# Two mixture-of-experts layers in fp32: expert weights multiplied unsplit, on column tiles of TensorE

## The reference

```
def expert_choice_ffn(h, w_router, w1, w3, w2):
    cap = max(1, EC_CAPACITY * T // N_EXPERTS)
    aff = jax.nn.softmax((h @ w_router).astype(jnp.float32), axis=-1)
    gate, idx = lax.top_k(jnp.swapaxes(aff, 1, 2), cap)
    xin = jax.vmap(lambda hb, ib: hb[ib])(h, idx)
    hid = jax.nn.silu(jnp.einsum('becd,edf->becf', xin, w1)) * jnp.einsum('becd,edf->becf', xin, w3)
    y = jnp.einsum('becf,efd->becd', hid, w2) * gate[..., None].astype(h.dtype)
    return jax.vmap(lambda yb, ib: jax.ops.segment_sum(
        yb.reshape(-1, D), ib.reshape(-1), num_segments=T))(y, idx)
```

## Time and profile before

| | us |
|---|---|
| median of 3 runs (4937.42 to 4945.94) | 4940.01 |
| the profiled execution | 4945.59 |
| its span, first to last instruction | 4943.9 |
| PE busy | 4181.3 |
| DVE busy | 2556.5 |
| ACT busy | 1902.5 |
| POOL busy | 1369.3 |
| granted TensorE clock, mean | 0.903 |
| raw loads, of 750.91 MB moved in all | 384 x 1 MB |

### The profile page before, as it was taken

How to read it: one execution, slowest core, us unless ns; L and a number is a source line. 1 busy time by engine, 2 the same in 40 slices (tenths; PEclk the granted TensorE clock), 3 DMA queues, 4 the chain that set the end, 5 groups by cost and what they waited for, 6 DMA issues and landing times. The chain is left out here.

```text
span 4943.9 us, 57028 instructions
## 1 busy us (share of the span) xinstructions
PE 4181.3 (85%) x23791; PEld 2752.6 (56%) x23791; DVE 2556.5 (52%) x3270; ACT 1902.5 (38%) x2614; POOL 1369.3 (28%) x814
## 2 busy tenths in 40 slices
PE   8988869999978956388996688887898998898998
PEld 4546546566644434277884556654445764455763
DVE  2215436777763037655534399898555331455321
ACT  2114216676643147333340276675114211123211
POOL 2200027686650012200002186676100210001210
PEclk9999979999999977657896799998999999999999
DMA  5330126888863138633322198897211221301321
GB/s 214 128 116 31 54 74 244 300 314 291 280 242 142 43 137 279 197 96 89 89 79 109 69 351 321 314 340 284 99 43 50 106 83 34 108 34 62 108 79 41
DMA packets 410482, 750.91 MB, mean 152 GB/s; under 512 B 67280, under 2 KB 143424, under 8 KB 410224
## 3 DMA queue, kind: packets, MB, share of 16 engines
q1 hardware_dynamic: 398816, 705.14, 40.8%
q0 software_dynamic: 11408, 42.13, 2.4%
HBM read 684.26 MB, written 62.94 MB: 151 GB/s over the span
## 5 line engine op out<-in xcount | busy, mean ns | idle before, releaser
L75 POOL TENSOR_TENSOR whl<-raw,whl 128x512 fp32r<-128x512 f32 x384 | 947.3, 2487 | 489.6 <-ACT whl L72 489.1
L75 DVE TENSOR_TENSOR whl<-raw,whl 128x1536 fp32r<-128x1536 f32 x384 | 871.2, 2292 | 135.7 <-ACT whl L72 132.5
L72 ACT ACTIVATE whl<-raw 128x2048 fp32r<-128x2048 f32 x384 | 730.4, 1915 | 288.7 <-PE ps L62 174.4
L62 PE MATMUL ps<-whl,xp 128*96 128x512 f32 (+2 forms) x2560 | 652.4, 406 | 77.9 <-DVE whl L75 41.5
L62 PEld LDWEIGHTS ps<-whl,xp 128*96 128x96 f32 (+2 forms) x2560 | 409.9, 165 | 301.1 <-DVE whl L75 73.1
L62 PE MATMUL ps<-c,hT 128*128 128x512 f32 (+2 forms) x1024 | 420.0, 565 | 5.1 <-ACT hT L72 2.8
L62 PE MATMUL ps<-whl,hidT 128*96 128x512 f32 (+2 forms) x1280 | 337.8, 415 | 60.9 <-DVE whl L75 45.1
L62 PE MATMUL ps<-wp,hp 128*128 128x512 f32 x1536 | 360.3, 396 | 20.2 <-DVE wp L75 20.2
L62 PE MATMUL ps<-a,nahT 128*128 128x512 f32 x768 | 338.5, 597 | 5.6 <-ACT nahT L72 5.2
L62 PEld LDWEIGHTS ps<-wp,hp 128*128 128x128 f32 x1536 | 290.8, 189 | 87.1 <-issue 27.3
L62 PEld LDWEIGHTS ps<-c,hT 128*128 128x128 f32 x1024 | 192.2, 192 | 200.0 <-issue 192.3
(11 more groups left out here) (468 smaller groups left out, 6251.9 us busy)
## 6 DMA issues: line engine op xcount, KB each, us to landing
raw<-in_moe_w_dram SPq DMA_DIRECT2D x384, 1024.0 KB, 5.2
c<-in_w_in_dram SPq DMA_DIRECT2D x28, 2048.0 KB, 9.2
a<-in_ada_w_dram SPq DMA_DIRECT2D x16, 2048.0 KB, 13.1
b<-in_ada_w_dram SPq DMA_DIRECT2D x8, 2048.0 KB, 9.9
a<-in_na_w_qkv_dram SPq DMA_DIRECT2D x6, 2048.0 KB, 19.1
c<-in_w_branch_dram SPq DMA_DIRECT2D x16, 512.0 KB, 4.2
c<-in_w_out_dram SPq DMA_DIRECT2D x4, 2048.0 KB, 9.0
c<-in_w_ple_gate_dram SPq DMA_DIRECT2D x4, 2048.0 KB, 8.0
```

The costliest lines, as they stand in the source:

```text
L62: return self.e.matmul(out, lhsT, rhs, start=start, stop=stop, skip_group_check=True) if self.e is not None else self
L72: return self.e.activation(*a, **k) if self.e is not None else self
L75: return self.e.tensor_tensor(*a, **k) if self.e is not None else self
```

## The change

Both layers now run one `moe_experts`, with the same quarters of 256 x 1024, and `pairs_experts` goes. The weights are not split: PE multiplies raw itself, in fp32, and the ring of raw (six tiles in layer 0, twelve in layer 1) is freed by PE's own count. The 64 latent tokens of an expert are multiplied by two column halves at once: columns 0 to 511 of the weight into partitions 0 to 63 and columns 512 to 1023 into partitions 64 to 127 of one bank. The 32 context tokens of layer 0 take four such tiles of 32 partitions and 256 columns each. With that, hid is 128 x 512 and no fold is needed, and POOL has nothing in the stage. Weighing by slot and by gate row comes into one operation on DVE (Yw, Ycw); Yw is split for an fp32r scatter, context results stay fp32 (Yc, Sc). The residual is loaded into acc ahead, so the scatter adds onto it. acc is the tile mx (layer 0) or hx (layer 1), into which the route loaded x before; the last groups are of two experts each. Layer 0's result stays in mx: `rw_norm` reads it there, rw_project's SP stores it to xl for the readout, and mx is then used again as kk and for scratch. The route of layer 0 now makes wslot too.

```diff
-class Halves:
+class Quarters:
...
-        self.src = [w[ex][h * 512:h * 512 + 512, n * 512:n * 512 + 512] for what, ex in self.order
-                    for n in range(2) for w in ws[what] for h in range(2)]
+        self.src = [w[ex][256 * q:256 * q + 256, :] for what, ex in self.order for w in ws[what] for q in range(4)]
...
-            e.wait_ge(*P.dve.at(self.name, 'low', u - self.nr))
-            e.wait_ge(*P.pool.at(self.name, 'low', u - self.nr))
-        n = self.src[u].shape[1]
-        to = self.raw[:, u % self.nr].rearrange("p a b -> p (a b)").rearrange("p (k n) -> p k n", n=n)
-        e.dma_start(to, self.src[u].rearrange("(k p) n -> p k n", p=128)).then_inc(*self.sig[u % self.nr].inc(self.name, u))
+            e.wait_ge(*self.P.pe.at(self.name, 'quarter', u - self.nr))
...
-                e.wait_ge(*P.dve.at(name, 'low', u))
-                out = P.psum[0:M, bank[p], :]
-                for k in range(4):
-                    kk = 4 * h + k
-                    if k == 3:
-                        e.wait_ge(*P.pool.at(name, 'low', u))
-                    e.matmul(out, x[:, kk, 0], hi(u)[:, k, :], (h, k) == (0, 0), False)
-                    e.matmul(out, x[:, kk, 0], lo(u)[:, k, :], False, False)
-                    ins = e.matmul(out, x[:, kk, 1], hi(u)[:, k, :], False, (h, k) == (1, 3))
...
+def moe_experts(P, I, l, mod, srcs, acc, name, chunks, nch, H, xinT, affT, posn, pix, bcc, posr, wslot, idr):
...
+                e.wait_ge(*H.loaded(u))
+                W = H.raw[:, u % H.nr]
                 for k in range(2):
+                    kk = 2 * q + k
+                    for t in range(2):
+                        X = xinT[:, kk, ex, 0:64] if kind == 'A' else hidT[:, ex % 2, kk]
+                        ins = e.matmul(P.psum[half(t), bank[0], :], X, W[:, k, cols(t if kind == 'A' else swap(t, ex))], kk == 0, kk == 7)
+                    for j in range(4 if two else 0):
+                        X = xinT[:, kk, ex, 64:96] if kind == 'A' else hicT[:, ex % 2, kk]
+                        ins = e.matmul(P.psum[part(j), bank[1], 0:256], X, W[:, k, blk(j)], kk == 0, kk == 7)
                 ins.then_inc(*P.pe.inc(name, 'quarter', u))
...
+                e.scalar_tensor_tensor(out=Yw[:], in0=P.bank(name, 'p', 'B', ex, 0), scalar=wslot[:, ex:ex + 1], in1=gl[:, ex % 2, :],
+                                       op0=MUL, op1=MUL).then_inc(*P.dve.inc())
...
-        e.wait_ge(*s_res.at(name, 'residual'))
-        for s, ch in enumerate(chunks):
-            for i in ch:
-                e.wait_ge(*P.dve.last())
-                e.tensor_tensor(acc[:, i, :], acc[:, i, :], xo[:, nch + s], MUL).then_inc(*P.dve.inc())
-                e.wait_ge(*P.dve.last())
-                e.tensor_tensor(acc[:, i, :], acc[:, i, :], xo[:, i], ADD).then_inc(*P.dve.inc(name, 'result', i))
...
+                if u == H.nr + 1:
+                    fence(P, e, k_('route'))
                     e.wait_ge(*gate_out(P, l, 1))
+                    for t in range(2):
+                        for ex in range(2):
+                            n = swap(t, ex)
+                            e.dma_start(gl[half(t), ex, :], bc(mod[l, 0, 5120 + n * 512:5632 + n * 512], 64)).then_inc(*s_gate.inc())
+                    for j in range(4 if two else 0):
+                        e.dma_start(gc[part(j), :], bc(mod[l, 1, 5120 + j * 256:5376 + j * 256], 32)).then_inc(*s_gate.inc())
+                    s_gate.name(name)
+                    for s, (src, ch) in enumerate(zip(srcs, chunks)):
+                        e.dma_start(acc[:, ch[0]:ch[-1] + 1], src.rearrange("(c p) n -> p c n", p=128)).then_inc(*s_res[s].inc(name))
...
+GROUPS = ((0, 1, 2, 3), (4, 5, 6, 7), (8, 9, 10, 11), (12, 13), (14, 15))
...
-            e.wait_ge(*s_x[c // 2].at('rw'))
+            e.wait_ge(*ready(c))
             e.wait_ge(*P.act.last())
-            e.activation(junk[:], x[:, c, :], ACT.Square, accum_out=ss[:, c:c + 1]).then_inc(*P.act.inc('rw', 'square', c))
+            e.activation(junk[:], acc[:, c, :], ACT.Square, accum_out=ss[:, c:c + 1]).then_inc(*P.act.inc('rw', 'square', c))
...
+                if (i, hs) == (2, 0):
+                    for c in range(4):
+                        e.wait_ge(*ready(c))
+                        e.dma_start(xl[c * 128:c * 128 + 128, :], acc[:, c, :]).then_inc(*s_xl.inc())
+                    s_xl.name('rw')
                 ring.fetch(e, R[2 * i + hs], I[w][0][:, hs * 512:hs * 512 + 512], nk)
...
-            moe(P, I, 0, mod, [xl[1], xc[1]], [xl[2], xc[2]], [64, 32], 'moe0', 'na_out', [(P.sig("na_out"), 'na')])
+            x = P.sb([128, 6, D], name="mx", ctx=b)
+            moe(P, I, 0, mod, [xl[1], xc[1]], x, [64, 32], 6, 'moe0', 'na_out', [(P.sig("na_out"), 'na')])
             with ExitStack() as c:
                 ring = Ring(P, 4, "b", c)
-                rwkv(P, I, mod, [xl[2], xc[2]], [xl[3]], ring, ('moe0', 'experts'), [(P.sig("moe0_out"), 'out')])
+                rwkv(P, I, mod, x, lambda c: P.dve.at('moe0', 'result', c), xl[2], [xl[3]], ring, ('moe0', 'experts'))
         x = P.sb([128, 4, D], name="hx")
-        moe_pairs(P, I, 1, mod, xl[3], x, [64], 'moe1', 'rw_readout', [(P.sig("rw_out"), 'rw')])
+        moe(P, I, 1, mod, [xl[3]], x, [64], 12, 'moe1', 'rw_readout', [(P.sig("rw_out"), 'rw')])```

PE at the first products of layer 0 (sel,hl gathers the tokens; aff,sel makes wslot; whl,xp and raw,xinT are product A; ident,hid turns hid). Before:

```order
L62 MATMUL ps<-sel,hl 128x512 x160
L62 MATMUL ps<-whl,xp 96x512 x132
L66 MATMUL ps<-ident,hid 128x96 x4
L62 MATMUL ps<-whl,xp 96x512 x12
L66 MATMUL ps<-ident,hid 128x96 x4
L62 MATMUL ps<-whl,xp 96x512 x48
L62 MATMUL ps<-whl,hidT 96x512 x36
```

More of the change, by code:

```diff
@@ L1235, in moe_route, with moe_plan @@
     d.close()
-def moe_plan(order, nch, two, nh, nhalves):
+GROUPS = ((0, 1, 2, 3), (4, 5, 6, 7), (8, 9, 10, 11), (12, 13), (14, 15))
+def moe_plan(order, nch):
     plan, tasks, done = [], [], set()
[L1241 to L1303, removed]
@@ L1543 @@
-class Quarters(Halves):
-    def __init__(self, P, I, l, name, raw):
-        super().__init__(P, I, l, name, raw)
-        ws = {'A': (I['moe_w1'][l], I['moe_w3'][l]), 'B': (I['moe_w2'][l],)}
-        self.src = [w[ex][256 * q:256 * q + 256, :] for what, ex in self.order for w in ws[what] for q in range(4)]
-GROUPS = ((0, 1, 2, 3), (4, 5, 6, 7), (8, 9, 10, 11), (12, 13, 14), (15,))
-def pairs_plan(order, nh, nquarters):
-    plan, tasks, done = [], [], set()
-    count = {'split': 0, 'quarter': 0}
+    quarters = itertools.count()
@@ L1566, in product, with turn @@
         for q in range(4):
[L1567 to L1572 removed]
+            plan.append(('quarter', next(quarters), q, p))
             tick()
[L1575 to L1576 removed]
+    def turn(ex):
+        plan.append(('gate', ex, 1))
         yield
[L1578 to L1587 removed]
+        plan.append(('turn', ex))
+        done.add(ex)
     def keep(ex):
@@ L1666, in pe @@
+    plan = moe_plan(H.order, nch)
+    s_res, s_gate = [P.sig(f"moe{s}_in") for s in range(len(srcs))], P.sig("moegt_in")
+    k_ = lambda *a: (name,) + a
+    cols = lambda n: slice(n * 512, n * 512 + 512)
+    half = lambda t: slice(64 * t, 64 * t + 64)
+    part = lambda j: slice(32 * j, 32 * j + 32)
+    blk = lambda j: slice(256 * j, 256 * j + 256)
+    pair = lambda ex: ex % 4 // 2
+    swap = lambda t, ex: t ^ ex % 2
     def pe(e):
@@ L1702, in pe @@
                 for f in free:
                     e.wait_ge(*f)
[L1704 to L1709 removed]
+                for j in range(4):
+                    ins = e.turn(P.psum[:, b, j * 128:(j + 1) * 128], hid[:, j * 128:(j + 1) * 128], P.ident)
@@ L1783, in act @@
+                for t in range(2):
+                    e.activation(Y[half(t), pair(ex), swap(t, ex), 0, :], Yw[half(t)], ACT.Copy).then_inc(*P.act.inc())
+                P.act.name(name, 'keep', ex)
+                if two:
+                    for j in range(4):
+                        e.activation(Yc[part(ex % 4), blk(j)], Ycw[part(j)], ACT.Copy).then_inc(*P.act.inc())
+                    P.act.name(name, 'keptc', ex)
         P.end(k_('experts'), P.act)
@@ L1857, in pool @@
         fence(P, e, k_('route'))
-        for what, *a in plan:
-            if what == 'split':
-                u = a[0]
-                e.wait_ge(*P.act.at(name, 'high', u))
-                e.tensor_tensor(flat(lo(u))[:, 1536:2048], raw(u)[:, 1536:2048], flat(hi(u))[:, 1536:2048].bitcast(F32), SUB).then_inc(*P.pool.inc(name, 'low', u))
         P.end(k_('experts'), P.pool)
@@ L1934, in rw_norm @@
     pr = P.sb([104, 128], name="rwpr", ctx=d)
[L1935 removed]
+    s_pr = P.sig("rwpr_in")
     def turned(lat, ctx):
```

666 lines of the change are left out of this document (191 added, 475 removed).

## The result

The changed kernel takes **4755.4 us** (median of 4 runs, 4743.4 to 4762.8) against 4938.7 (4 runs): a ratio of 0.9626, 95% interval 0.9600 to 0.9652. It is faster by 183 us; the forecast was 321 us less, and its range ended at 4735. The profiled execution took 4743.4 us, with a span of 4741.7, against 4945.6 and 4943.9 before; it lies 12.0 us under its kernel's median, and the one before lay 6.9 over its own.

What follows compares the result with a forecast made beforehand. Loads were to bind both expert stages at 2.76 us a quarter; gains of 175 us (first layer) and 146 us (second) took the profiled 4945.6 to 4625, and 5.6 for the median gave 4619 us, range 4535 to 4735.

Steps and rivals of the forecast that it cites:

- An fp32 matmul of 128 x 512 takes 222.8/512 = 0.435 us (oT): PE's price for an unsplit product, read from the oT row; 0.44 us taken for a pair of 64 x 512.
- PE needs 2.2 us a quarter: First layer at full clock: 1.9 us of products plus 0.33 of other work, under the loads' 2.76 us.
- less than two, in place of the three: Unsplit fp32 products on PE cost less than two fp32r matmuls, 0.435 us against 0.246 each, before column tiles.
- raw,xinT matmuls of 64 x 512 at 0.22 us of busy time each: Expert stages: busy time of each such matmul on PE, a sign that the forecast is right.
- A change of shape costs 0.13 with its uncovered weights: First layer, PE switching between 64 x 512 and 32 x 256 tiles twice per k: 2 x 0.13 us per k.
- Loads at 380 GB/s: Both expert stages: weight loads from a queue that is always full run at 380 GB/s, 2.76 us a quarter.
- rival 2: Both expert stages: loads run at 411 GB/s, 2.55 us a quarter, 77 us less, 4542 us; chance 0.15.
- Rival 1: Both expert stages: the queue doesn't improve with depth, 347 GB/s, 3.02 us a quarter, 4716 us; chance 0.13.
- Rival 3: First layer: PE binds through its clock; 4701 us at half and half, 4887 always at half; chance 0.12.
- Rival 4: First layer: column tiles of 512 fp32 columns run one after the other, 4.4 us a quarter, 4919 us; chance 0.03.
- Rival 5: First layer: half clock holds and shape changes cost more; gain gone at 0.30 each, 5017 us at 0.4; chance 0.03.
- Start of layer 0 two us and a half earlier: First product of layer 0 at 768.5 instead of 770.95, with 64 slot-weight matmuls ahead at 0.03 us each.

Runs made afterwards that it cites:

- lone tile: Changed kernel, but in layer 0 only the first of each pair of 64 x 512 matmuls is run after a product's first k; 4752.5 us (one run).
- one pass: Changed kernel, but experts' products of both layers read only the upper 16 bits of each number as bf16; 4561.1 us, ratio 0.9231.

## Why the prediction was wrong, and where it was right

**The step that failed** is "An fp32 matmul of 128 x 512 takes 222.8/512 = 0.435 us (oT)". The 512 are records, and the matmuls are 256. From it came "1.9 us" for a quarter's product and "PE needs 2.2 us a quarter", under the loads' 2.76, and so the verdict that both stages come to be bound by loads. With 0.86 for a pair and 0.43 for four, the same working gives 2 x (0.86 + 0.43 + 0.29) + 0.33 = 3.5 us, over the loads; measured 3.56. So PE and not the loads binds the first layer, and 186 x (3.56 - 2.76) = 149 of the 156 us by which that line missed are what a quarter takes beyond my 2.76, nearly all of it by this step (PE's other work adds 0.40 in place of 0.33). It takes the sum from 4619 to 4768; measured 4755. That the two are close is in part luck: 10 us more came in the first layer and at its start, 40 less in the other lines (23 of them in layer 1, by faster loads), and 18 more because the two profiled executions lie on different sides of their medians. In layer 1 the price was as wrong, 2.0 us for 1.2, and it did no harm, since 2.0 is still under the loads' 2.56.

The Trainium skill has the rule that would have stopped it: "FP8 and Floating Point Precision", TensorE Precision Notes, says that true FP32 takes four passes through the array. The traces agree: 0.87 us for 512 fp32 columns against 0.246 for an fp32r matmul, 3.5 to 1. By that rule "less than two, in place of the three" is wrong on its face: unsplit fp32 costs PE more than the three fp32r terms (0.87 against 0.74), and what keeps PE's bill in the first layer near the old one (685 against 649 busy us) is the column tiles, which take a k from 2 x 0.87 = 1.74 to 1.58 where the three fp32r terms took 6 x 0.246 = 1.48.

My signs were blind to this. "raw,xinT matmuls of 64 x 512 at 0.22 us of busy time each" came out as 244.0/1024 = 0.24 in the second layer, nearly right, because the sign had the same unit as the mistake:

```profile
L62 PE MATMUL ps<-raw,xinT 128*64 128x512 f32 x1024 | 244.0, 606 | 50.5 <-DMA raw<-in_moe_w_dram 50.1 <-PE ps L62 0.4
```

The signs that did tell were the DMA share (0.82 for 0.97) and PE without waits for raw.

**Point by point:**
- Column tiles run as one, two of 64 and four of 32: right, and at 512 columns too (lone tile).
- A change of shape costs 0.13 with its uncovered weights: right, 0.118 on average.
- PE's other work, 0.33 us a quarter: 3.56 - 3.16 = 0.40.
- Loads at 380 GB/s: too low. In the second layer it is 409, for 400 us on end, which is rival 2's rate. Rival 2 came true in that one layer, where 169 us were gained for the forecast 146; in the other PE hid it. The 8 us row at 411 showed what the queue holds; why the 20 us rows I preferred (376 and 393) are lower isn't shown, and at shares of 1.00 and 1.04 it wasn't idle time.
- Rival 1 (347): refuted; so is, for this core, the 358 GB/s by which I gave its estimate. "Perfetto Trace Analysis" of the Trainium skill, in its note on HBM over 100%, says that a core alone may go above that share up to its 16 DMA engines' 435; the runs agree with 409.
- Rival 3 (PE binds through its half clock): the stage is PE's, but at a clock of 0.99; and where the clock did fall, to 0.67 with one pass, a k was cheap enough for the loads to hide it. Its two halves didn't occur together.
- Rival 4 (column tiles in series, 4.4 us a quarter, 4919): its mark, PE busy throughout, was there, its mechanism was not.
- Rival 5 (slower): not seen; it asked for the half clock and 0.30 a change, and the clock was 0.99 and a change 0.118 at it.
- Path from the last scatter to rwx: 10.5 forecast, 8.3 measured. Store of xl at no cost: not tested alone; the stage behind it got no longer.
- Start of layer 0 two us and a half earlier: no, 0.5 later. Most of that is the same miscount: my 0.03 us was for a record, the 64 matmuls of slot weights ahead of the first product have 128, and they take 4.3 us in place of 2:

```profile
766.70 4.34 PE L62 MATMUL ps<-aff,sel 128*64 128x1 f32 x128
```

## What to carry to other kernels

Before a duration from a trace is multiplied by a count from the program, set the trace's count beside the program's: where an instruction leaves several records, the mean of a record is a fraction of its price, and any sign that is built on the same row can't show the mistake. A split into low and high parts pays PE back (here 0.74 us for three fp32r matmuls against 0.87 for one in fp32); taking it out frees the other engines and costs PE, so it helps the stage that isn't PE's (here the second) and leaves the one that is. And when PE does bind, the order of matmuls with different tile shapes is worth looking at: grouping them gave 87 us for no change in what is computed.

## What the runs showed of the hardware that I had not expected

- Weight loads of 1 MB on one queue ran at 409 GB/s for 400 us on end with a ring of twelve, and at 399 with a ring of four.
- An fp32 product is recorded as two instructions for matmul and weight load alike; an fp32r or bf16 one as one.
- A stage at a granted clock of 0.57 can be as short as one at 0.99, where loads bind: 484 us with one pass (bf16), 489 in fp32.
